# Two transformer blocks on one core: the last tile of both down products is computed by token halves

## The reference

```python
def first_block(x, ...):
    ...                                    # attention, x of the first join
    h = rms_norm(x, norm_ffn_pre[l])
    f = (jax.nn.silu(h @ w_gate[l]) * (h @ w_up[l])) @ w_down[l]     # 2816 -> 1024
    x = x + rms_norm(f, norm_ffn_post[l])
    return x

def second_block(x, ..., final_g):
    h = rmsnorm(x, norm1_g[layer])
    proj = jnp.einsum('bsd,de->bse', h, w_in[layer])                 # q, k, v, forget gate, u
    ...                                    # causal attention with forget gates, pooled means of u, w_out
    h2 = rmsnorm(x, norm2_g[layer])
    x = x + jnp.einsum('bsf,fd->bsd', jax.nn.silu(h2 @ w_gate) * (h2 @ w_up), w_down[layer])
    return rmsnorm(x, final_g)
```

## Time and profile before

| what | value |
|---|---|
| median of 3 runs | 1219.95 us (1219.86 to 1220.07) |
| the profiled execution's own time | 1218.82 us |
| its span, first to last instruction | 1216.6 us |
| TensorE busy | 1137.2 us, 93% |
| VectorE, ScalarE, GpSimd busy | 668.3, 502.8, 142.6 us |
| mean granted TensorE clock | 0.982 |
| TensorE in the chain that ended last | 80% |
| stores of the result | 8 of 256 KB, 2.3 us from issue to landing |

### The profile page before, as it was taken

One profiled execution on the slowest core, in us unless ns is written; L12 is line 12 of the kernel. 1 busy time (PEld: TensorE's weight loads), 2 busy tenths in 40 slices (PEclk: granted clock), 3 DMA queues, 4 the chain that ended last, 5 costly groups with the idle time before them and its releaser, 6 DMA issues.

```text
span 1216.6 us, 15011 instructions
## 1 busy us (share of the span) xinstructions
PE 1137.2 (93%) x5276; PEld 925.1 (76%) x5276; DVE 668.3 (55%) x1096; ACT 502.8 (41%) x844; POOL 142.6 (12%) x154
## 2 busy tenths in 40 slices
PE   6897968979999999999979998799999999999995
PEld 5675857878888888888856886577888888888884
DVE  6776786777444444433368687744544444433332
ACT  6786676454333232322234366733433323332221
POOL 1375663000000000000011002200000000000001
PEclk9999989999999999999989998999999999999998
DMA  7311100413322232222222221012322222223211
GB/s 259 117 52 45 52 27 1 157 52 111 114 91 99 86 103 103 98 100 98 102 77 74 83 104 36 1 48 92 121 87 94 95 103 99 90 104 101 100 41 69
DMA packets 31469, 106.10 MB, mean 87 GB/s; under 512 B 4032, under 2 KB 4672, under 8 KB 31296
## 3 DMA queue, kind: packets, MB, share of 16 engines
q1 hardware_dynamic: 31088, 104.99, 24.8%
q10 hardware_dynamic: 336, 0.52, 0.2%
HBM read 100.78 MB, written 2.10 MB: 85 GB/s over the span
## 4 chain that ended last, share of the span: by engine, by line
PE 80%; DVE 9%; ACT 6%; issue 3%; DMA 0%; ACTq 0%; POOL 0%; DVEq 0%; SPq 0%
PE bank L466 23%; PE bank L467 23%; PE bank L468 23%; PE bank L912 1%; PE bank L902 1%; DVE wl L388 1%; PE bank L863 1%; PE bank L865 1%; PE bank L864 1%; DVE q L1121 1%; ACT wh L380 1%; DVE pr L1010 1%; DVE xres L1658 1%; DVE ta L1656 1%; ACT pth L1144 1%
## 5 line engine op out<-in xcount | busy, mean ns | idle before, releaser
L388 DVE TENSOR_TENSOR wl<-raw,wh 128x1024 fp32r<-128x1024 f32 x181 | 223.4, 1234 | 304.3 <-ACT wh L380 304.0
L466 PE MATMUL bank<-hh,wh 128*128 128x512 f32 x904 | 358.8, 397 | 17.5 <-DVE hl L1664 15.6
L380 ACT ACTIVATE wh<-raw 128x1024 fp32r<-128x1024 f32 x181 | 191.2, 1058 | 441.8 <-PE bank L468 299.2
L468 PE MATMUL bank<-hh,wl 128*128 128x512 f32 x904 | 354.3, 392 | 0.0
L467 PE MATMUL bank<-hl,wh 128*128 128x512 f32 x904 | 354.2, 392 | 0.0
L466 PEld LDWEIGHTS bank<-hh,wh 128*128 128x128 f32 x904 | 171.3, 190 | 57.2 <-issue 16.5
L467 PEld LDWEIGHTS bank<-hl,wh 128*128 128x128 f32 x904 | 171.5, 190 | 36.3 <-issue 1.4
L468 PEld LDWEIGHTS bank<-hh,wl 128*128 128x128 f32 x904 | 171.0, 189 | 36.4
L468 PE MATMUL bank<-gh,wl 128*128 128x512 f32 x352 | 139.0, 395 | 0.0
L466 PE MATMUL bank<-gh,wh 128*128 128x512 f32 x352 | 139.0, 395 | 0.0
L467 PE MATMUL bank<-gl,wh 128*128 128x512 f32 x352 | 139.0, 395 | 0.0
(11 more groups left out here) (231 smaller groups left out, 1503.3 us busy)
## 6 DMA issues: line engine op xcount, KB each, us to landing
raw<-weights SPq DMA_DIRECT2D x181, 512.0 KB, 3.2
xres<-x_t SPq DMA_DIRECT2D x8, 512.0 KB, 6.5
sw<-ta SPq DMA_DIRECT2D x36, 64.0 KB, 2.0
out_t<-final SPq DMA_DIRECT2D x8, 256.0 KB, 2.3
rope<-angles SPq DMA_DIRECT2D x1, 1024.0 KB, 10.7
sw<-ta ACTq DMA_DIRECT2D x4, 64.0 KB, 3.0
wp<-pool_weights ACTq DMA_DIRECT2D x1, 256.0 KB, 3.4
mats_raw<-matrices SPq DMA_DIRECT2D x1, 128.0 KB, 8.8
```

Of the source, the lines that this page charges most:

```text
L380: act.activation(wh[:, j, :, :], raw[:, j, :, :], ACT.Copy).then_inc(high_split, 1)
L388: v.tensor_tensor(wl[:, j, :, :], raw[:, j, :, :], wh[:, j, :, :].bitcast(F32), ALU.subtract)\
L466: pe.matmul(bank[:, :], wh[:, slot, b, :], ah[:, k, :], start=first and n == 0, stop=False)
L468: ins = pe.matmul(bank[:, :], wl[:, slot, b, :], ah[:, k, :], start=False, stop=last and n == len(blocks) - 1)
```

## The change

For both down products the last output tile (tile 7) is computed by token halves. All 22 blocks are multiplied for tokens 0 to 255 into its own bank, then all 22 again for tokens 256 to 511 into bank 4, the weights staying in their slots until the second pass. The sum of squares of the first half is made in bank 5 after four blocks of the second.

Behind the first block, scale, update and split of `x` go by halves, in the way of the earlier join, whose helpers now take a `Join`. In2's first four tiles are computed by halves: three chunks as the feature tiles of the first half come, the fourth chunk, then the second half. The second half's sum stands after five feature tiles, the sum for norm1 behind all of it. The squares for norm1 go to `sqs2`, and VectorE adds them instead of GpSimd. The other tiles are taken by TensorE three tiles ahead of their reading, into six banks (`in_bank`) instead of four. The copies of k's low part for the other head are written by ScalarE (`act_other_keys`) instead of VectorE.

At the end, the first half of the result is scaled by VectorE and stored in four transfers during the second half; the second half goes out in five. GpSimd takes no part in it. The loops of the down products are written out.

```diff
-VECTOR_LAST, GPSIMD_LAST = (0, 1, 2, 3, 4), (5, 6, 7)
...
+        def down_last(name, half):
+            return (banks[(TILE0[name] + KT - 1) % 4], banks[4])[half]
+
+        def down_sum(pe, full, halves, half, bank):
+            n = HALVES[half]
+            pe.wait_ge(full.added, KT - 1)
+            pe.matmul(bank[:, n], ones[:, :], acc[:, n], start=True, stop=False)
+            pe.wait_ge(halves[half].squared, 1)
+            pe.matmul(bank[:, n], ones[:, :], sw[:, (KT - 1) % 2, n], start=False, stop=True).then_inc(halves[half].summed, 1)
+
+        def in_bank(ph, m):
+            return banks[(0, 1, 2, 3, 6, 7)[m % 6]]
+
         def pe_in(pe, ph):
             n = len(ph.tiles)
+            pe.wait_ge(bank_read, ph.t0 - 1)
+            pe_halves(pe, ph.c0, ph.t0, ph.h, 0, [(k, j) for k in range(5) for j in range(3)])
+            down_sum(pe, n_fo, n_fh, 1, banks[6])
+            pe_halves(pe, ph.c0, ph.t0, ph.h, 0, [(k, j) for k in range(5, KT) for j in range(3)] + [(k, 3) for k in range(KT)])
+            pe_halves(pe, ph.c0, ph.t0, ph.h, 1, [(k, j) for k in range(SPLIT) for j in range(4)]
+                      + [(k, j) for j in range(4) for k in range(SPLIT, KT)])
             for m in range(n + 4):
...
+                if 1 <= m < n - 3:
+                    f = m + 3
+                    slot_wait(pe, ph.c0 + f)
+                    if f >= 6:
+                        pe.wait_ge(bank_read, ph.t0 + f - 5)
+                    products(pe, in_bank(ph, f), (ph.c0 + f) % RING, range(KT), hh, hl, 0, True, True).then_inc(used, 1)
...
+        def splits_at(ph, m):
+            n = len(ph.tiles)
+            return [m + RING + 2] if m + RING + 2 < n else [m + RING] if n <= m + RING < n + RING else []
...
+        def act_other_keys(act, ph, m):
+            i = ph.tiles[m][2]
+            act.wait_ge(ph.fin.low, ph.low_count(m))
+            for par, own, other in pair():
+                ins = act.activation(ph.kl[par][other, i, :], ph.kl[par][own, i, :].bitcast(F32), ACT.Copy)
+            ins.then_inc(ph.keys, 1)
...
+        def vec_down1(v):
...
+            vec_last(v, 0)
+            v.wait_ge(n_fh[0].ready, 1)
+            for k in range(2):
+                vec_scale(v, join2, k, 0)
+                vec_update(v, join2, k, 0)
+            vec_split(v, i0 + 1)
+            for k in range(2, KT):
+                vec_scale(v, join2, k, 0)
+                vec_half_low(v, join2, k - 2, 0)
+                vec_update(v, join2, k, 0)
+                if k == 3:
+                    vec_split(v, i0 + 2)
+                    vec_last(v, 1)
+                if k == 4:
+                    vec_split(v, i0 + 3)
+            vec_half_low(v, join2, 6, 0)
+            vec_second_half(v, join2, n_fh[1].ready)
+            vec_split(v, i0 + RING)
+            vec_sum_squares(v, join2)
...
+        def act_down1(act):
...
+            act_last(act, 0)
+            act_half_rstd(act, n_fh[0], 0, banks[5])
+            act_split(act, i0 + 1)
+            for k in range(4):
+                act_half_h(act, join2, k, 0)
+                if k == 1:
+                    act_split(act, i0 + 2)
+            act_last(act, 1)
+            act.dma_start(wp[:, :, :], wpool_in).then_inc(wpool_loaded, 16)
+            act_split(act, i0 + 3)
+            for k in (4, 5):
+                act_half_h(act, join2, k, 0)
+            act_half_rstd(act, n_fh[1], 1, banks[6])
+            for k in (6, 7):
+                act_half_h(act, join2, k, 0)
+            for k in range(KT):
+                act_half_h(act, join2, k, 1)
+            act_split(act, i0 + RING)
...
+        def pe_down(pe, name, gu, full, halves):
...
+            bank_free(pe, t0 + KT - 1)
+            for half in range(2):
+                n, bank = HALVES[half], down_last(name, half)
+                k0 = 0
+                for p in range(per):
+                    c = c0 + per * (KT - 1) + p
+                    if half == 0:
+                        slot_wait(pe, c)
+                    for b in range(DOWN[p]):
+                        if (half, p, b) == (1, 0, 4):
+                            down_sum(pe, full, halves, 0, banks[5])
+                        k = k0 + b
+                        pe.matmul(bank[:, n], wh[:, c % RING, b, :], gh[:, k, n], start=k == 0, stop=False)
+                        pe.matmul(bank[:, n], wh[:, c % RING, b, :], gl[:, k, n], start=False, stop=False)
+                        ins = pe.matmul(bank[:, n], wl[:, c % RING, b, :], gh[:, k, n], start=False, stop=k == FT - 1)
...
+        def vec_down2(v):
...
+            vec_last_x(v, 0)
+            vec_final(v, 0)
+            vec_last_x(v, 1)
+            vec_final(v, 1)
...
         @block.sync
...
+            for k in range(0, KT, 2):
+                store(sp, 0, k, 2)
+            store(sp, 1, 0, 2)
+            store(sp, 1, 4, 2)
+            store(sp, 1, 7, 1)
```

More of the change, by code:

```diff
@@ L436, in low_count @@
             def low_count(self, m):
-                return sum({"q": 2, "k": 4}.get(self.tiles[f][1], 1) for f in self.fins[:self.fin_count(m)])
+                return sum({"q": 2, "k": 2}.get(self.tiles[f][1], 1) for f in self.fins[:self.fin_count(m)])
             def low_total(self):
@@ L1759, in act_gate_up @@
                     act_split(act, gu.c0 + RING + 2 * r + 2, i)
[L1761 to L1775 removed]
+        down_half = {name: sem(name + "_first_half") for name in ("down1", "down2")}
@@ L1799, in pe_out2, with vec_last_x, vec_final @@
                 products(pe, banks[(t0 + j) % 4], (c0 + j) % RING, range(KT), mh, ml, 0, True, True).then_inc(used, 1)
+        def vec_last_x(v, half):
+            n = HALVES[half]
+            if half == 0:
+                v.wait_ge(down_half["down2"], 1)
+            else:
+                v.wait_ge(used, CHUNK0["down2"] + len(DOWN) * KT)
+            v.tensor_tensor(xres[:, KT - 1, n], down_last("down2", half)[:, n], xres[:, KT - 1, n], ALU.add).then_inc(bank_read, 1)
+        def vec_final(v, half):
+            n = HALVES[half]
+            v.wait_ge(n_eh[half].ready, 1)
+            v.wait_ge(x_gained, KT + half)
+            for k in range(KT):
+                v.tensor_tensor(final[:, k, n], final[:, k, n], rstd[:, n], ALU.mult).then_inc(x_final, 1)
@@ new lines, in vec_down2 @@
+        def vec_down2(v):
+            c0, t0, per = CHUNK0["down2"], TILE0["down2"], len(DOWN)
+            for k in range(KT - 1):
+                for p in range(per):
+                    if (k, p) != (0, 0):
+                        vec_split(v, c0 + per * k + p + RING)
+                v.wait_ge(used, c0 + per * (k + 1))
+                v.tensor_tensor(xres[:, k, :], banks[(t0 + k) % 4][:, :], xres[:, k, :], ALU.add).then_inc(bank_read, 1)
+                add_square(v, n_fin, k, acc)
+            vec_last_x(v, 0)
+            vec_final(v, 0)
+            vec_last_x(v, 1)
+            vec_final(v, 1)
@@ new lines, in act_last_x, with act_down2 @@
+        def act_last_x(act, half):
+            n = HALVES[half]
+            act.wait_ge(bank_read, TILE0["down2"] + KT + half)
+            act.wait_ge(n_fin.added, KT - 2)
+            act.activation(sw[:, (KT - 1) % 2, n], xres[:, KT - 1, n], ACT.Square).then_inc(n_eh[half].squared, 1)
+            act.activation(final[:, KT - 1, n], xres[:, KT - 1, n], ACT.Copy, scale=col("final", KT - 1)).then_inc(x_gained, 1)
+            act_half_rstd(act, n_eh[half], half, banks[5 + half])
+        def act_down2(act):
+            c0, t0, per = CHUNK0["down2"], TILE0["down2"], len(DOWN)
+            for k in range(KT - 1):
+                for p in range(per):
+                    if (k, p) != (0, 0):
+                        act_split(act, c0 + per * k + p + RING)
+                act.wait_ge(bank_read, t0 + k + 1)
+                act_square(act, n_fin, k, xres[:, k, :])
+                act.activation(final[:, k, :], xres[:, k, :], ACT.Copy, scale=col("final", k)).then_inc(x_gained, 1)
+            act_last_x(act, 0)
+            act_last_x(act, 1)
+            store(act, 1, 2, 2)
+            store(act, 1, 6, 1)
@@ L1801, in build, with store @@
+        def store(eng, half, k, tiles):
+            n = HALVES[half]
+            eng.wait_ge(x_final, KT * half + k + tiles)
+            eng.dma_start(out[:, k:k + tiles, n], final[:, k:k + tiles, n]).then_inc(out_stored, 16)
         wpool_split = Split("wpool")
```

336 lines of the change are left out of this document (156 added, 180 removed).

## The result

The changed kernel took 1216.47 us (median of 19 runs, 1214.92 to 1218.92), the kernel before 1220.82 beside it (19 runs, 1217.39 to 1225.03): ratio 0.9964, 95% interval 0.9955 to 0.9974, some 4.4 us less (3.2 to 5.5). The forecast was 1211.6 with a range of 1208.6 to 1215.6: the sign is right, the size half of what was forecast, and the time lies above the range.

A forecast was written before the change was run, and what follows sets the result against it. TensorE, busy 93% of the span, was taken as the bound. Span 1216.6 - 4.1 (join) - 4.3 (end) = 1208.2; execution 1210.4, with the median 1.13 above: 1211.6 us, range 1208.6 to 1215.6.

The forecast's parts named there:

- The waits of the join: Behind the first down product, TensorE's waits at the half-width tiles and sums: 0.5, 1.1, 1.15 and 3.6, together 6.3 us.
- The clock: After TensorE's 3.6 us wait for norm1's sum, the clock falls to half for 3.3 us: 1.6 us lost.
- Net 4.1 at the join: Behind the first down product: 5.7 us less from last down tile to fifth projection, with 1.6 lost to the clock.
- if the rest of the projections stays bound by TensorE: Condition on the 4.1 us gain: from 651.60 to 735.00 TensorE was busy 81.04 of 83.40, VectorE 65.94.
- TensorE has four whole tiles in front of VectorE and six banks to put them in: In the projections, cover for the scaling factor coming at about 654.1 instead of 651.6.
- The two low parts per k tile that move from VectorE to ScalarE: In the projections' k tiles: this work lies beside matmuls and costs nothing.
- VectorE takes over in the projections: Rival: VectorE bounds the projections, the join costs 2.5 us, time 1218.2; chance 0.10, shared with no effect.
- Half width: Split matmuls of both down tiles and the projections: 0.240 us for a 256-column pair against about 0.23 whole.
- The end: From the second down product's last tile to the span's end: halved scalings and stores give 4.3 us less.
- T: At the end, the start of the last matmul of the last down tile's first half, put at 1193.81.
- 3.96 us lay between the last issue and the end of the span: At the end: the time after the last store's issue, taken from the profile before and kept unchanged.
- GpSimd now has none, so they don't slow each other: Final scalings of the second half: eight on VectorE at 0.34 us each; before, five took 6.30 beside GpSimd's three.

The follow-up runs named there:

- keys_order: The changed kernel with ScalarE's copies of the next k tile's high part ahead of the last one's low-part copies; ratio 0.9920 to the kernel before.
- sum_first: The changed kernel with VectorE adding the squares for norm1 before the split of the fifth weight chunk; ratio 0.9923 to the kernel before.
- sum_behind: The changed kernel with the sum for norm1 behind the fifth projection in TensorE's list; ratio 0.9926 to the kernel before.
- aux_first: The changed kernel with v transposes and pool products ahead of the same step's projection in TensorE's list; ratio 0.9937 to the kernel before.
- keys_vector: The changed kernel with both low copies of k written by VectorE again, none by ScalarE; ratio 0.9949 to the kernel before.
- join_only: The changed kernel with the old end: whole last tile, one sum, scalings on VectorE and GpSimd, eight stores; ratio 1.0010 to the kernel before.
- all3: The changed kernel with k high-part copies ahead, squares before the fifth split, transposes and pool products ahead; 1205.15 us, ratio 0.9878 to before.

## Why the prediction was wrong

- **The waits of the join**: right. Forecast 0.5, 1.1, 1.15 and 3.6; measured 0.27, 0.73, 0.86 and 3.57.
- **The clock**: right, with a size that differs between executions. It fell at the wait for the sum and not in the half-width stream; 3.4 us at half cost 1.7, forecast 1.6, but in keys_order the same wait cost 0.9 more. sum_first and sum_behind show it from the other side: without the wait, no fall.
- **"Net 4.1 at the join"**: TensorE is 4.11 earlier at the end of in2. Right as far as TensorE's own list goes.
- **"... if the rest of the projections stays bound by TensorE. It was ... yet TensorE has four whole tiles in front of VectorE and six banks to put them in. The two low parts per k tile that move from VectorE to ScalarE lie beside matmuls: nothing."** This step failed: the projections didn't stay bound by TensorE, which waited 7.48 us before the scores where none was forecast. The scores came 2.5 later than before instead of 4.1 earlier, an error of 6.6. I had weighed VectorE by its mean over the whole stretch, 17.5 us free in 83, and that free time isn't where the work is: before, 2 us of it lay in each of the last steps, when VectorE waits for TensorE, and those go first when TensorE runs ahead. The tiles ahead that I took for cover are the debt: what TensorE has ahead, VectorE still has to do when TensorE is through, and VectorE can't follow sooner, because transposes and weight slots that it waits for stand behind those tiles in TensorE's list (13.1 us of waits for the transposes; aux_first 2.27 of the scores). And two instructions moved from a busy engine to a free one weren't free, since a wait and a queue order came with them (keys_order 3.9 of the wait, keys_vector 3.3 of the scores), against the "nothing" of the forecast.
- **The rival "VectorE takes over in the projections"** had the outcome to the digit (join costs 2.5) and 0.10 of the chance, shared with another. That is luck. The factor did come 2.7 later (first tile scaled at B+49.7 against B+47.1), but sum_first and sum_behind show that the scores don't hang on it, and VectorE isn't the bound by its load; the late v transposes and the chain of ScalarE and VectorE were not in the rival.
- **Half width**: a pair of 256-column matmuls took 0.237 in the down product and 0.240 in in2, beside 0.233 and 0.227 for a whole one; forecast 0.240. The rule of the Trainium skill ("TensorE: Matmul & The Clock Gate", section "Back-to-back issue gap") has 2.5 ns more for a pair; the rows, which decide, have 4 and 13.
- **The end**: forecast 4.3, measured 5.5 against the one profile of before and 4.7 against join_only. All steps up to the last issue hold (first scaling forecast at T+11.6, with T = 1198.90 it is T+11.64; last issue T+14.5, measured T+14.44). The mis-sized term is "3.96 us lay between the last issue and the end of the span", which was 2.96: carried over from one execution with a slow landing, where the same end has 3.22 in join_only. "GpSimd now has none, so they don't slow each other" was said of the second half alone; that it is worth 2.3 to 3.1 by itself was not seen.
- The sum of the measured terms, +2.5, -5.5 and -0.3, is -3.3 (-2.6 with the end of join_only), and the runs say -4.4 (-3.2 to -5.5). Whether the 1.1 to 1.8 between is anything but the profiles' variation stays open.

## What to carry to other kernels

When one engine is let run ahead of its consumer, count the consumer's work that is left when the producer is through, at the end of the stage and not by its mean load, and look for what the consumer needs from the producer behind the tiles ahead. A wait that is removed can uncover a second one of the same length, as aux_first did. An instruction moved to an idle engine brings its wait along: put it behind everything there that others wait for, here `act_finish` before `act_other_keys`. And where VectorE and GpSimd share elementwise work on operands in SBUF, try VectorE alone first.

## What the runs showed that I had not expected

- Eight 512-wide multiplications on VectorE alone took 4.90 us (0.68 each, overlapping), five beside GpSimd's three 6.30 (1.74 each while both worked).
- At the same wait of 3.57 us the clock fell 0.7 us after its end in the changed kernel, for 3.4 us, and 1.6 us before its end in keys_order, for 6.8 us. The wait costs its length and a part that differs between executions. At the 1.36 in all3 it didn't fall.
- Two profiles of the same old end differ by 0.75 us, all of it behind the last issue.
- 256-column matmuls of the down product with `gh` have a pitch of 0.119, those of in2 0.120.
